# Hybrid mLSTM and sparse-attention decoder layer: gates and convolutions moved under the first projection, page numbers read ahead, the last norm on VectorE alone

## The chip, the core and the metric

One core of a Trainium2 chip runs the whole layer as one program. Its engines each have a queue of their own and meet by semaphores: TensorE (PE in rows; PEld is its weight load), VectorE (DVE), ScalarE (ACT), GpSimd (POOL) and SyncE (SP), which here only issues DMAs. ScalarE and GpSimd issue DMAs too. The metric is the device time of one execution in microseconds (us), lower is better.

## The reference

One inference step of a decoder layer for two groups of tokens with the same weights: a prompt of 1024 tokens, and 8 sampled sequences of 4 new tokens each with 4096 tokens of paged cache. 1056 tokens in all go through every projection.

```
h = rmsnorm(x, nrm[0])
xm, v, ig, fg, og, qn, kvc, kvs, kvw, gn, ga, gb = split_in(h @ p['w_in'])
hm, C, n, m, mconv_new = mlstm_mixer(xm, v, ig, fg, og, mconv, C0, n0, m0, p)
on, new_rows, new_win = nsa_mixer(...)        # compressed, selected, sliding window
merged = sigmoid(ga) * (hm @ p['w_up_m']) + sigmoid(gb) * (on @ p['w_up_n'])
x = x + rmsnorm(merged @ p['w_out'], nrm[1])
...                                            # cross-attention into 256 memory tokens
x = x + rmsnorm((gelu(u) * (h @ p['f_wg'])) @ p['f_wd'], nrm[5])

def mlstm_mixer(xm, v, ig, fg, og, conv_buf, C0, n0, m0, p):
    xc, conv_new = causal_dwconv(xm, conv_buf, p['m_conv_w'], p['m_conv_b'])   # width 4
    xc = silu(xc)
    q, k = xc @ p['m_wq'], xc @ p['m_wk'] * M_HD ** -0.5                       # per head
    i_pre, log_f = ig + b[0], log_sigmoid(fg + b[1])
    ...                                        # chunkwise recurrence, output gate
```

The compressed branch of the sparse attention puts every 32 cached keys and values of each sequence through a two-layer network, which reads the key and value halves of all 32 pages of each of the 8 sequences. Everything is in fp32.

## The kernel before

The layer is a row of stages, each a block of programs for the five engines. A stage ends when all its engines and DMAs are through, and the next begins with none of its own DMAs issued. Inside a stage the order on each engine is written out by hand, and semaphores (`S["..."]`) order the engines.

**front.** The first norm and the input projection. Large products are made exact enough by splitting both operands in a high and a low half and taking three products (`split_product`). The token-major part of the projection comes first. Then 12 chunks of 128 feature rows: for chunk `j`, SP loads the weights into half `j % 2` of `ring`, ScalarE makes the high half (`chunk_high`), VectorE the low half (`chunk_low`), TensorE multiplies, and VectorE drains the product (`drain_chunk`) into `zm` for chunks 0 to 3, the convolution's input, or into `zn`. The halves of chunk 0 lie in `zhalf`, those of the others in two places in `wlow`, which is the same memory as `hm`.

**mlstm.** SP loads gate bias, convolution taps, saved states, the query and key weights of the 4 heads (`wqk`) and the norm's gains. VectorE adds the gate bias and makes the log of the forget gate in four steps, with ScalarE's exponential and logarithm between. It convolves feature tile after feature tile (`convolve(c)`, prompt and sample tokens), with ScalarE's Silu behind each. TensorE projects a head (`project_head`) when its Silu is done, ScalarE copies queries and keys, TensorE turns the keys (`turn_keys`) and ScalarE copies them (`turned_keys`). In between VectorE makes the running maxima, then the carry from tile to tile. ScalarE makes the output gates' sigmoids and then the weights (`weights_ready`). With the weights the scan begins: 8 tiles, in which TensorE, ScalarE, VectorE and GpSimd take turns.

**states and blocks** (`sab_` in names). The mLSTM of the samples, the bias vector of the attention in four parts (`bias_part`, from a one-hot table in `ring`), and the compressed blocks: the prompt's own (`own_first`, which reads pairs that VectorE and ScalarE turn), and those of the 8 sequences, each a first layer for keys and one for values (`first(n, kv)`). Sequence `n` uses buffer `n % 2` of 32 pages. SP, ScalarE and GpSimd load 12, 9 and 11 of them (`load`); for a page an engine first reads its number from `pages` into a register (`value_load`), then issues a DMA of 128 KB. They read four numbers and issue four DMAs in turn, after waiting for the buffer: for sequences 2 and on, the first layers of sequence `n - 2` (`layer1_ready`), for sequence 1 both own first layers (`own1_ready`), since its buffer holds their pairs.

**Sparse attention, merge, output and query, memory, cross-attention** follow and are not touched.

**ff.** The feed-forward, and the last norm on three groups of 352 tokens. For each group TensorE sums squares and spreads the factor row, ScalarE takes the root and copies the row, and the output is scaled by it and added to `x`: VectorE does 6 of the 8 feature tiles (`scale3`, `add3`), GpSimd the other 2 (`finish`). Group 0 is finished while TensorE works on group 2, groups 1 and 2 after the last matmuls.

## Time and profile before

| | us |
|---|---|
| three runs | 2480.99, 2485.36, 2490.33 |
| median | 2485.36 |
| profiled execution | 2488.14 |
| its span in the trace | 2484.9 |

Five stretches of the span, from the trace: busy time of the engines, the clock granted to TensorE as a share of its full 2.4 GHz, and the mean busy share of the 16 DMA engines.

| stretch, us | stage | TensorE | VectorE | ScalarE | GpSimd | clock | DMA |
|---|---|---|---|---|---|---|---|
| 0 to 300 | front | 288.83 | 63.77 | 62.17 | 0.84 | 1.00 | 0.21 |
| 300 to 426 | mlstm | 77.20 | 80.05 | 54.55 | 18.17 | 0.83 | 0.13 |
| 426 to 579 | states and blocks | 119.11 | 33.09 | 18.91 | 47.48 | 0.77 | 0.81 |
| 579 to 2440 | attention to feed-forward | 1781.12 | 885.70 | 549.39 | 351.20 | 0.98 | 0.26 |
| 2440 to 2485 | end of ff | 20.06 | 29.82 | 8.70 | 15.94 | 0.68 | 0.27 |

Over the span TensorE is busy for 2286.3 us (92%), VectorE 1092.4 (44%), ScalarE 693.7 (28%) and GpSimd 433.6 (17%). A row of a timeline gives start and duration, the engine, the line of the program, the operation with what it writes and reads, and in brackets the idle time of the engine before it and what ended it. SPq and ACTq are the queues of an engine that issue DMAs.

### The profile page before, as it was taken

The page shows a single profiled execution, that of the slowest core. Times are in us where ns is not written, and L with a number is a line of the kernel's source. Part 1 is how long each engine was busy: PE and PEld are TensorE (multiplying, and loading weights), DVE is VectorE, ACT ScalarE, POOL GpSimd, SP SyncE. Part 2 cuts the span into 40 slices and gives each one's busy share as a digit, 9 for nine tenths or more (in the row PEclk, how much of TensorE's full clock was granted, in tenths as well). Part 3 has the DMA queues.
Part 4 walks back from the last instruction along what each step waited for, and adds up shares of the span by engine and source line. Part 5 has one row for each costly group of instructions (what it writes and reads, how often), then busy time and mean ns, then how long its engine had stood idle before and what let it go on. Part 6 is the DMA issues. An engine that isn't in the chain of part 4 may idle for free. (4 is left out here: it accounts for less than half of the span.)

```text
span 2484.9 us, 40696 instructions
## 1 busy us (share of the span) xinstructions
PE 2286.3 (92%) x15977; PEld 2076.0 (84%) x15977; DVE 1092.4 (44%) x2456; ACT 693.7 (28%) x1394; POOL 433.6 (17%) x381
## 2 busy tenths in 40 slices
PE   8999875876998998999899999998999999999995
PEld 7799745774555568999899968898999999999995
DVE  2211266134666674132228115457655555552336
ACT  4210153112565563011134003443111111121123
POOL 0000012330322302212011100111221221222223
PEclk9999978788999999999999999998999999999997
DMA  3211111888543523111211055212111111111312
GB/s 141 93 48 51 23 1 43 278 283 317 182 154 103 173 81 108 51 61 47 100 68 35 34 208 227 69 49 73 60 43 52 43 51 43 42 41 45 113 40 77
DMA packets 114298, 233.20 MB, mean 94 GB/s; under 512 B 23394, under 2 KB 76291, under 8 KB 110675
## 3 DMA queue, kind: packets, MB, share of 16 engines
q1 hardware_dynamic: 88250, 183.32, 21.9%
q0 software_dynamic: 10368, 28.33, 3.5%
q10 hardware_dynamic: 15490, 18.97, 2.2%
q8 instruction: 126, 2.06, 0.3%
q14 instruction: 64, 0.52, 0.1%
HBM read 207.28 MB, written 27.47 MB: 94 GB/s over the span
## 5 line engine op out<-in xcount | busy, mean ns | idle before, releaser
L88 PE MATMUL psum<-x_half_high,ff_half 128*128 128x352 f32 x3240 | 790.8, 324 | 10.8 <-POOL ff_half L69 4.9
L88 PEld LDWEIGHTS psum<-x_half_high,ff_half 128*128 128x128 f32 x3240 | 567.0, 189 | 12.8 <-POOL ff_half L69 5.9
L88 PE MATMUL psum<-h_again_low,ff_half 128*128 128x352 f32 x1176 | 378.0, 321 | 0.0
L69 POOL TENSOR_TENSOR ff_half<-ring,ff_half 128x1024 fp32r<-128x1024 f32 (+2 forms) x85 | 177.1, 2083 | 752.5 <-ACT ff_half L3068 752.5
L88 PEld LDWEIGHTS psum<-h_again_low,ff_half 128*128 128x128 f32 x1176 | 222.0, 189 | 0.0
L88 PE MATMUL psum<-merged_high,oq_half 128*128 128x352 f32 x768 | 189.4, 327 | 9.3 <-DVE oq_half L69 7.7
L3068 ACT ACTIVATE ff_half<-ring 128x1024 fp32r<-128x1024 f32 (+2 forms) x88 | 78.0, 888 | 428.2 <-PE psum L88 407.2
L88 PE MATMUL psum<-mid_low,ff_half 128*128 128x352 f32 x516 | 167.0, 324 | 0.0
L88 PEld LDWEIGHTS psum<-merged_high,oq_half 128*128 128x128 f32 x768 | 135.8, 191 | 9.9 <-DVE oq_half L69 8.0
L88 PE MATMUL psum<-h_high,in_half 128*128 128x352 f32 x528 | 126.1, 321 | 0.0
L88 PE MATMUL psum<-x_half_high,mg_w_high 128*128 128x352 f32 x384 | 124.0, 323 | 2.1 <-ACT gated L2135 1.2
L88 PE MATMUL psum<-h_again_low,mg_w_high 128*128 128x352 f32 x384 | 123.1, 321 | 0.0
L88 PE MATMUL psum<-x_half_high,mg_w_low 128*128 128x352 f32 x384 | 123.0, 320 | 0.0
L1761 ACT ACTIVATE na_pt<-psum 128x512 f32<-128x512 f32 (+1 forms) x170 | 86.8, 544 | 94.6 <-PE psum L1636 80.7
L1456 POOL DMA_DIRECT2D na_kv<-in_pool x128 | 70.4, 551 | 226.4 <-PE psum L1663 159.4
L1636 PEld LDWEIGHTS psum<-consts,na_p 128*128 128x128 f32 x528 | 57.6, 144 | 58.7 <-DVE na_p L1919 37.6
L88 PE MATMUL psum<-in_half,h_high 128*128 128x512 f32 (+3 forms) x360 | 102.8, 371 | 0.0
L3392 DVE TENSOR_TENSOR h_again<-h_again,psum 128x352 f32<-128x352 f32 x96 | 49.8, 520 | 119.6 <-PE psum L88 119.5
L1741 ACT ACTIVATE na_p<-na_p,na_nm 128x640 f32<-128x640 f32 (+7 forms) x128 | 92.8, 727 | 28.5 <-DVE na_nm L1777 28.1
L88 PEld LDWEIGHTS psum<-mid_low,ff_half 128*128 128x128 f32 x516 | 98.1, 190 | 0.0
L1636 PE MATMUL psum<-consts,na_p 128*128 128x128 f32 x528 | 80.6, 287 | 15.7 <-DVE na_p L1919 13.0
L855 PE MATMUL psum<-sab_kv,sab_w 128*64 128x128 f32 x1024 | 70.7, 305 | 24.8 <-DMA sab_kv<-in_pool 22.4
(559 smaller groups left out, 4215.8 us busy)
## 6 DMA issues: line engine op xcount, KB each, us to landing
na_kv<-in_pool SPq DMA_DIRECT2D x128, 128.0 KB, 3.5
na_kv<-in_pool POOLq DMA_DIRECT2D x128, 128.0 KB, 4.0
sab_kv<-in_pool SPq DMA_DIRECT2D x96, 128.0 KB, 4.4
mg_w<-in_w_merge SPq DMA_DIRECT2D x15, 768.0 KB, 4.4
sab_kv<-in_pool POOLq DMA_DIRECT2D x88, 128.0 KB, 4.5
ring<-in_f_wu SPq DMA_DIRECT2D x22, 512.0 KB, 3.3
ring<-in_f_wg SPq DMA_DIRECT2D x22, 512.0 KB, 3.2
sab_kv<-in_pool ACTq DMA_DIRECT2D x72, 128.0 KB, 4.5
```

Source lines behind the costliest of these rows:

```text
L69: return engine.tensor_tensor(low, x, high.bitcast(F32), ALU.subtract)
L88: ins = nc.tensor.matmul(out, w[a], x[b], start=first and n == 0, stop=last and n == 2)
L855: last = nc.tensor.matmul(psum[g * HD:(g + 1) * HD, bank, 0:width], w1[:, kv, j, :], rows(g, j), start=(j == 0), stop=(j == CB // 2 - 1))
L1456: eng.dma_start(kv[m % 2][:, b, 2 * PAGE * p:2 * PAGE * (p + 1)], A["pool"][ds(g, 1), :, 2 * PAGE:4 * PAGE].rearrange("a p x -> (a p) x")) ...
L1636: last = nc.tensor.transpose(out[:, c:c + P], src, K["ident"][:, :])
L1741: ins = nc.scalar.activation(x, x, ACT.Exp, bias=nm[:, b, g, i:i + 1], scale=-1.0, accum_out=sums[:, b, g:g + 1])
L1761: nc.scalar.activation(dst, psum[:, 4 + n % 2, 0:2 * m * P], ACT.Copy).then_inc(S["copied"], 1)
L3068: nc.scalar.activation(half(u)[:, 0, 0:n], ring[:, u % 2, 0:n], ACT.Copy).then_inc(S["w_high"], 1)
L3392: ins = nc.vector.tensor_tensor(z[:, f, col(g)], z[:, f, col(g)], bank(v), ALU.add)
```

## The change

**In front.** Gate bias and taps are loaded at the start. The halves of even chunks lie in `zhalf`, those of odd ones in `extra`, so that `hm` is free. VectorE does the gates under chunks 1, 3 and 6, and the convolution of prompt tokens of tile `c` under chunk `4 + c`; ScalarE does the exponential behind the high half of chunk 4, the logarithm behind that of chunk 6 and the four Silus behind those of chunks 7 to 10. At the end SP loads the head weights into the free half of `ring`, where states and blocks finds them too. The small gate tensors and the taps get an earlier place in memory. **In mlstm** the waits for all this go. The sample tokens are convolved all at once (`convolve_sample`) behind the running maxima, and their Silu stands behind the output gates. **In states and blocks** the load of the head weights goes, the one-hot table is loaded after the pages of sequence 0 and the samples' projections, and `bias_part(0)` moves behind `last_entries`. `load` reads three numbers at a time for sequence 0, and for the others all its numbers before it waits for the buffer. **In ff** GpSimd's `finish` goes, and VectorE scales in two halves of 4 tiles and adds all four pairs.

```diff
     def chunk_half(j):
-        if j == 0:
+        if j % 2 == 0:
             return zhalf[:, KD - 2, 0:KD * P], zhalf[:, KD - 1, 0:KD * P]
-        s = 2 * ((j - 1) % 2)
-        return tuple(wlow[:, s + i].rearrange("p n w -> p (n w)") for i in range(2))
+        return tuple(extra[:, i].rearrange("p n w -> p (n w)") for i in range(2))
...
+            sp.wait_ge(S["chunk_low"], nchunk - 1)
+            sp.dma_start(heads_weights(ring), A["m_wqk"]).then_inc(S["wqk_loaded"], 16)
...
             for j in range(2, nchunk):
                 chunk_high(j)
+                if j == 4:
+                    act.wait_ge(S["gate_steps"], 2)
+                    nc.scalar.activation(tmp[:, :, :], tmp[:, :, :], ACT.Exp).then_inc(S["gate_exp"], 1)
+                if j == 6:
+                    act.wait_ge(S["gate_steps"], 3)
+                    nc.scalar.activation(tmp[:, :, :], tmp[:, :, :], ACT.Ln).then_inc(S["gate_ln"], 1)
+                if 7 <= j < 7 + MH:
+                    act.wait_ge(S["conv_ready"], j - 6)
+                    nc.scalar.activation(hm[:, j - 7, 0:TP], hm[:, j - 7, 0:TP], ACT.Silu).then_inc(S["silu_done"], 1)
...
-            for j in range(3):
+            for j in range(2):
                 chunk_low(j)
...
+            under = {1: gate_inputs, 3: one_more, 6: log_forget}
             for j in range(nchunk):
                 drain_chunk(j)
-                if 1 <= j < nchunk - 2:
+                if j < nchunk - 2:
                     chunk_low(j + 2)
+                if j in under:
+                    under[j]()
+                if 4 <= j < 4 + MH:
+                    convolve(j - 4)
...
             def project_head(h):
-                pe.wait_ge(S["silu_done"], h + 1)
...
-            pe.wait_ge(S["steps"], 4)
             nc.tensor.matmul(psum[:, GATE, 0:R], K["tri"][:, :], lf[:, 0:NTILE, :].rearrange("p t h -> p (t h)"),
...
-            pe.wait_ge(S["loaded"], 80)
             project_head(0)
...
+            act.wait_ge(S["conv_ready"], 1)
+            nc.scalar.activation(hm[:, :, TP:T], hm[:, :, TP:T], ACT.Silu).then_inc(S["silu_done"], 1)
             turned_keys(3)
...
         def load(eng, n, first, count, done):
-            if n == 1:
-                eng.wait_ge(S["own1_ready"], 2)
-            if n >= 2:
-                eng.wait_ge(S["layer1_ready"], 2 * (n - 1))
-            for at in range(first, first + count, 4):
-                some = range(at, min(at + 4, first + count))
+            step = count if n else 3
+            for at in range(first, first + count, step):
+                some = range(at, min(at + step, first + count))
                 page = [eng.value_load(pages[0:1, n * NPAGE + e:n * NPAGE + e + 1], min_val=0, max_val=N["n_pool"] - 1) for e in some]
+                if n == 1:
+                    eng.wait_ge(S["own1_ready"], 2)
+                if n >= 2:
+                    eng.wait_ge(S["layer1_ready"], 2 * (n - 1))
...
-            sp.dma_start(wqk[:, :, :, :], A["m_wqk"]).then_inc(S["wqk_loaded"], 16)
...
+            load(sp, 0, 0, SP_N, loaded)
+            sp.wait_ge(S["qk_ready"], 1)
             sp.dma_start(onehot, A["onehot"]).then_inc(S["vec_loaded"], 16)
-            load(sp, 0, 0, SP_N, loaded)
...
             spread_row(a, "diag_a_ready", "arow_ready")
-            bias_part(0)
             own_first(0)
             scores()
             spread_row(M, "diag_m_ready", "mrow_ready")
             last_entries()
+            bias_part(0)
             bias_part(1)
...
+            halves3 = (slice(4, 8), slice(0, 4))
...
-                    scale3(0)
-                    add3(0, pairs[0:3])
+                    scale3(0, halves3)
+                    add3(0, pairs)
             add_square3(7, 2)
-            scale3(1)
+            scale3(1, halves3[0:1])
             mean3(2)
-            add3(1, pairs[0:1])
+            scale3(1, halves3[1:2])
             factor3(2)
-            add3(1, pairs[1:3])
-            scale3(2)
-            add3(2, pairs[0:3])
+            add3(1, pairs)
+            scale3(2, halves3)
+            add3(2, pairs)
```

Order on VectorE. Before, the convolution of tile 0 in mlstm (`low` is the memory of `zm` and `hm`, `xs` and `ys` hold the sample tokens):

```order
L719 TENSOR_SCALAR low<-low,cw 128x1024
L720 TENSOR_SCALAR ys<-xs,cw 128x32
L723 SCALAR_TENSOR_TENSOR low<-low,cw 128x1021
L725 SCALAR_TENSOR_TENSOR ys<-xs,cw,ys 128x32
L723 SCALAR_TENSOR_TENSOR low<-low,cw 128x1022
L725 SCALAR_TENSOR_TENSOR ys<-xs,cw,ys 128x32
L723 SCALAR_TENSOR_TENSOR low<-low,cw 128x1023
L725 SCALAR_TENSOR_TENSOR ys<-xs,cw,ys 128x32
L727 COPY low<-ys 128x32
```

Now, in front under chunks 4 and 5 (L427 drains a chunk, L69 makes a low half):

```order
L427 SCALAR_TENSOR_TENSOR zn<-psum,fr_row 128x1056
L69 TENSOR_TENSOR zn_half<-ring,zn_half 128x1024
L475 TENSOR_SCALAR low<-low,cw 128x1024
L478 SCALAR_TENSOR_TENSOR low<-low,cw 128x1021
L478 SCALAR_TENSOR_TENSOR low<-low,cw 128x1022
L478 SCALAR_TENSOR_TENSOR low<-low,cw 128x1023
L427 SCALAR_TENSOR_TENSOR zn<-psum,fr_row 128x1056
L69 TENSOR_TENSOR tok_half<-ring,tok_half 128x1024
```

The prompt's part moved between a low half and the next drain; the sample's part stands alone later.

Order on ScalarE, in mlstm between the turned keys of head 2 and the weights (`ex`). Before:

```order
L693 ACT_TABLE_LOAD
L693 ACTIVATE branch_gates<-tokn 128x216
L696 ACTIVATE tokm<-tokm 128x512 x8
L696 ACTIVATE tokm<-tokm 32x512
L660 ACTIVATE kt<-psum 128x4x128 x2
L700 ACT_TABLE_LOAD
L700 ACTIVATE ex<-ex 128x128
```

Now:

```order
L725 ACT_TABLE_LOAD
L725 ACTIVATE branch_gates<-tokn 128x216
L728 ACTIVATE tokm<-tokm 128x512 x8
L728 ACTIVATE tokm<-tokm 32x512
L731 ACT_TABLE_LOAD
L731 ACTIVATE low<-low 128x4x32
L700 ACTIVATE kt<-psum 128x4x128 x2
L734 ACT_TABLE_LOAD
L734 ACTIVATE ex<-ex 128x128
```

A table load and the Silu of the sample columns came in ahead of the last turned keys.

Order on TensorE, at the head of states and blocks, from the first row spread to the first page layer (`sab_pairs` are the prompt's pairs, `sab_rel` is the bias table's factor, `sab_kv` a sequence's pages). Before:

```order
L990 MATMUL psum<-sab_tmp,consts 32x128
L998 MATMUL psum<-ring,sab_rel 8x512
L855 MATMUL psum<-sab_pairs,sab_w_3196 64x33 x32
L1041 MATMUL psum<-sab_qT,sab_kT 32x32 x4
L990 MATMUL psum<-sab_tmp,consts 32x128
L1045 MATMUL psum<-sab_Mb,consts 32x8
L998 MATMUL psum<-ring,sab_rel 8x512
L855 MATMUL psum<-sab_pairs,sab_w_3196 64x33 x32
L998 MATMUL psum<-ring,sab_rel 8x512 x2
L855 MATMUL psum<-sab_kv,sab_w_3196 64x128 x32
```

Now:

```order
L1014 MATMUL psum<-sab_tmp,consts 32x128
L879 MATMUL psum<-sab_pairs,sab_w_3197 64x33 x32
L1065 MATMUL psum<-sab_qT,sab_kT 32x32 x4
L1014 MATMUL psum<-sab_tmp,consts 32x128
L1069 MATMUL psum<-sab_Mb,consts 32x8
L1022 MATMUL psum<-ring,sab_rel 8x512 x2
L879 MATMUL psum<-sab_pairs,sab_w_3197 64x33 x32
L1022 MATMUL psum<-ring,sab_rel 8x512 x2
L879 MATMUL psum<-sab_kv,sab_w_3197 64x128 x32
```

The first bias part moved from ahead of the first own-key layer to behind the last entries.

## Rows read from the trace of the kernel before

**Rows 1.** Timeline, VectorE at the mLSTM's start (start us, us, engine, line, op).

```profile
308.08 0.23 DVE L765 TENSOR_TENSOR tokn<-tokn,gb 128x72 f32<-128x72 f32 x1 [7.33 <-DMA mnorm<-in_m_norm]
...
309.37 0.81 DVE L719 TENSOR_SCALAR low<-low,cw 128x1024 f32<-128x1024 f32 x1
...
310.43 1.28 DVE L723 SCALAR_TENSOR_TENSOR low<-low,cw 128x1021 f32<-128x1021 f32 x1
```

**Rows 2.** Timeline, ScalarE before the mLSTM's scan.

```profile
344.96 1.08 ACT L660 ACTIVATE kt<-psum 128x512 f32<-128x512 f32 x2
346.06 1.28 ACT L693 ACT_TABLE_LOAD   x1
347.36 0.38 ACT L693 ACTIVATE branch_gates<-tokn 128x216 f32<-128x216 f32 x1
...
354.68 0.31 ACT L700 ACTIVATE ex<-ex 128x128 f32<-128x128 f32 x1
```

**Rows 3.** Timeline, TensorE, first layers of the pages.

```profile
482.53 5.38 PE L855 MATMUL psum<-sab_kv,sab_w 128*64 128x128 f32 x64
...
506.94 5.42 PE L855 MATMUL psum<-sab_kv,sab_w 128*64 128x128 f32 x64 [6.48 <-DMA sab_kv<-in_pool]
...
519.41 3.71 PE L855 MATMUL psum<-sab_kv,sab_w 128*64 128x128 f32 x64 [0.60 <-DMA sab_kv<-in_pool]
...
524.78 3.71 PE L855 MATMUL psum<-sab_kv,sab_w 128*64 128x128 f32 x64
...
566.07 6.54 PE L855 MATMUL psum<-sab_kv,sab_w 128*64 128x128 f32 x64 [6.89 <-DMA sab_kv<-in_pool]
```

**Rows 4.** Windows of 5 us in states and blocks (busy by engine, PEclk, DMA share, GB/s).

```profile
530.00:535.00 5.00, 0.00 (x0) 0.00 (x0) 1.45 (x3) 0.00 (x0) 2.35 (x5) 0.59 1.04 345
545.00:550.00 5.00, 5.00 (x82) 4.71 (x80) 1.82 (x4) 0.37 (x1) 0.00 (x0) 1.00 0.36 117
```

**Rows 5.** Timeline, the last norm, on TensorE, VectorE and GpSimd.

```profile
2454.58 1.33 PE L2990 MATMUL psum<-consts,ff_acc 128*88 128x1 f32 x8 [3.93 <-DVE ff_acc L3400]
...
2463.52 3.90 DVE L3413 TENSOR_TENSOR h_again<-h_again,ff_row 128x704 f32<-128x704 f32 x2 [0.30 <-ACT ff_row L3130]
...
2467.45 2.24 DVE L3421 TENSOR_TENSOR low<-low,h_again 128x704 f32<-128x704 f32 x1
...
2469.70 1.65 DVE L3421 TENSOR_TENSOR low<-low,h_again 128x704 f32<-128x704 f32 x2
...
2476.30 3.84 DVE L3421 TENSOR_TENSOR low<-low,h_again 128x704 f32<-128x704 f32 x3
...
2466.02 2.93 POOL L3250 TENSOR_TENSOR low<-low,h_again 128x704 f32<-128x704 f32 x1
```

**Rows 6.** Timeline, VectorE's drains under the first projection's chunks.

```profile
195.39 1.26 DVE L411 SCALAR_TENSOR_TENSOR low<-psum,fr_row 128x1056 f32<-128x1056 f32 x1 [9.06 <-PE psum L88]
...
206.83 1.26 DVE L411 SCALAR_TENSOR_TENSOR low<-psum,fr_row 128x1056 f32<-128x1056 f32 x1 [9.06 <-PE psum L88]
```

**Rows 7.** Timeline, TensorE, heads of the mLSTM projected and turned.

```profile
323.04 3.67 PE L539 MATMUL psum<-low,wqk 128*128 128x512 f32 x8 [1.44 <-ACT qT L652]
326.55 1.04 PE L549 MATMUL psum<-consts,kT 128*128 128x128 f32 x8
...
337.50 6.50 PE L539 MATMUL psum<-low,wqk 128*128 128x512 f32 x8 [3.63 <-ACT qT L652]
```

**Rows 8.** Timeline, TensorE at the head of states and blocks.

```profile
431.10 0.64 PE L982 MATMUL psum<-low,sab_wqk 128*128 128x32 f32 x2 [8.13 <-DMA sab_wqk<-in_m_wqk]
...
443.45 3.63 PE L855 MATMUL psum<-sab_pairs,sab_w 128*64 128x33 f32 x64 [1.97 <-ACT sab_pairs L943]
...
456.11 1.87 PE L998 MATMUL psum<-ring,sab_rel 33*8 33x512 f32 x2 [0.68 <-ACT ring L1135]
```

**Rows 9.** Timeline, the DMA issues of pages on SP's and ScalarE's queue.

```profile
473.75 11.44 SPq L937 DMA_DIRECT2D sab_kv<-in_pool  x12
...
530.82 7.35 ACTq L937 DMA_DIRECT2D sab_kv<-in_pool  x9
```

146 lines of the change are left out of this document (65 added, 81 removed).

## Prediction

> **What bounds the kernel now.** I read the shares of the page first: TensorE is busy for 92% of the span, so there is a gain only where it waits. The table of the five stretches shows where: the two in the middle and the last. Then the timeline of each engine there, asking at each gap what ended it.
>
> Between the first projection and the scan of the mLSTM (300 to 359 us) VectorE first waits 7.33 us for a DMA issued at the stage's start, then works off the gates and four convolutions in series [rows 1], and TensorE can project a head only when its convolution is through. What ends this part is ScalarE: behind the turned keys of head 2 it loads a table, takes the gates' sigmoids, turns the last keys, loads the exponential's table and makes the weights [rows 2], for which the scan waits.
>
> In states and blocks (426 to 579) TensorE has 119 us of work in 153 and the DMA engines are 0.81 busy, so neither is full. Each sequence's 4.19 MB of pages come into one of two buffers, and its matmuls start when they are in: at 506.94 and, four sequences on, at 566.07, so 14.8 us each [rows 3]. The DMA rate swings between 345 and 117 GB/s [rows 4]: after a buffer comes free, each queue first reads page numbers.
>
> At the end VectorE's last two groups are one chain, started by the last projection tiles, and these tiles had waited 3.93 us for VectorE's work on the first group [rows 5].
>
> **Gates and convolutions under the chunks.** A chunk takes TensorE 11.44 us: so far apart lie VectorE's drains, and VectorE waits for 9.06 of it [rows 6]. To the drain of 1.26 and a low half of about as much comes at most one convolution, 0.81 + 3 x 1.28 = 4.65 us [rows 1], and items of 0.2: 7.2 in all. The low half stands ahead of the convolution, so the next chunk doesn't wait for it. Free, with 4 us to spare; without that cover it would be 19 us. ScalarE now waits for VectorE before the exponential, the logarithm and each Silu, with the next chunk's high half queued behind; each of these inputs is made at least one chunk before, so these waits and the three table loads lie in its idle time. The loads that moved into SP's queue (gate bias, taps, head weights) have nothing urgent behind them, and the head weights' half of the ring is free from chunk 10's low half on, 30 us before they are read.
>
> The new head: TensorE starts at 300.0 with the two cumulative products (about 1.1), then per head 3.67 us of projection and 1.04 of turns [rows 7]. ScalarE needs 3.1 per head (two copies of 1.0 and 1.08), so TensorE sets the pace: 300.0 + 1.1 + 4 x 3.67 + 3 x 1.04 + 0.6 of small turns = 319.5, and ScalarE ends the keys of head 2 at 320.6. Before, it ended them at 346.04 and the weights at 354.99 [rows 2], 8.95 later. Into that chain comes a Silu of the sample's columns with its table load, 1.28 + 0.28. Weights at 320.6 + 8.95 + 1.56 = 331.1: **23.9 us earlier**. VectorE isn't late: the running maxima are done by 308, the sample's convolution (some 21 small instructions) by 312, and its carry chain ends at about 324. The scan is untouched.
>
> Bounds: 26 if the small turns hide; below, TensorE at half clock throughout: a head then takes 6.50 [rows 7] and its turns double, 3.8 us more a head, 15 in all, which leaves 9.
>
> The Trainium skill, "ScalarE: Activation LUTs", section "What ACT_TABLE_LOAD costs", adds a drain of some 1.38 us to each load, 2.66 in all. The trace disagrees: behind the load at 346.06 the next activation starts at 347.36, 1.30 later [rows 2]. By the page the term would be 22.5.
>
> **States and blocks, its head.** TensorE no longer waits for the head weights, 426.4 instead of 431.10. But the first own-key layer waits for ScalarE's turned pairs until 443.45 [rows 8], and those stand behind 5 DMA issues and 9 pages on ScalarE's queue, as before: the 4.7 us go into a longer wait. Bias part 0, which filled that wait, now stands behind the last entries, on the path, and part 1 waits for its copy: 1.87 less 0.07 of overlap, and a wait of 0.68 like the one now ahead of part 3 [rows 8]. So the **first page layer is 2.5 us later**. SP's new wait, for the projections, has the one-hot table, the states and sequence 1's pages behind it; SP comes to it at about 443, and the projections are done at 435: nothing. The table then has 5 us to land.
>
> **Its pages.** SP's 12 pages took 11.44 us; ScalarE's 9 began 2.3 us after the buffer was free (528.49, then 530.82) and took 7.35 [rows 3, 9]. These 2.3 are four page numbers, 0.57 each. SP and GpSimd now read theirs ahead of the release: their first issue comes at once, and SP's 12 take (11.44 - 8 x 0.57) = 7 us. ScalarE comes to its reads only with the release, since the layer's activation stands ahead of them: its first page is later (9 x 0.57 = 5.1), its last at the same 10 us.
>
> The queues then issue faster than the engines move, and the rate is what the trace shows at its fullest, 345 to 348 GB/s, of which 345 has its row [rows 4]: 12.1 us for 4.19 MB. From release to start I take 0.5 + 12.1 + 2 to land = 14.6 (ScalarE's last page gives 10 + 4.5). Before, it was 19.0, from 482.53 + 5.38 to 506.94 [rows 3]. A warm sequence computes from 519.41 to 528.49, 9.1 [rows 3]. A pair needs the larger of 9.1 + 14.6 = 23.7 and 2 x 12.1 = 24.2, against 29.6. So sequence 3 starts at 487.9 + 14.6 = 502.5, 4.4 earlier, and sequence 7 four steps of 12.1 on, at 550.9, 15.2 earlier. Its first layer took 6.54 at half clock after a wait of 6.89 [rows 3]; after 2 us of waiting I take the 3.71 of a warm one, 2.8 less. 15.2 + 2.8 - 2.5 = **15.5 us**.
>
> Bounds: below, sequences stay 14.8 apart and only the bias counts: -2.5. Above, the 23.7 of the cycle and a hidden bias: 19.
>
> **The last norm.** Beside GpSimd's add, one of VectorE's pairs takes 2.24; alone, two take 1.65, so 0.83 each [rows 5]. Alone, a group is two scales of 1408 columns (1.55 each) and four adds: 6.4 us, where three quarters took 3.90 + 3.84 = 7.7. Group 0 ends 1.3 earlier, and TensorE's last tiles with it. Groups 1 and 2 took 2463.52 to 2480.14, 16.6; now 2 x 6.5 = 13.0, the factor row of group 2 (2.0 on TensorE, 0.5 on ScalarE) hidden behind the adds of group 1, which it wasn't. 1.3 + 3.6 less 0.3, as four stores now come faster than they drain: **4.6**. Bounds: 2.5 (only the contention goes) and 6.5 (TensorE's last 24 matmuls at full clock).
>
> Sum: 23.9 + 15.5 + 4.6 = 44.0. The profiled execution took 2488.14 us, 2484.9 of it span, and would take 2444.1. It lay 2.8 above the median of the runs, 2485.36; for the median I forecast 2441.
>
> **Rivals.** (a) The page reads were no cost: the pages come as fast as the engines move them. The Trainium skill, "DMA: Bandwidth & Descriptors", section "Issuing engines are not separate DMA queues", calls the sequencer's time to initiate usually small beside the DMA. In rows: sequences stay 14.8 apart, the term is -2.5, 2485.4 - 23.9 + 2.5 - 4.6 = 2459. Against it stand the 117 GB/s between loads [rows 4]. (b) TensorE stays at half clock in the new head of the mLSTM: 15 lost, 2456. Against it: it leaves the chunks at full clock and rests 1.6 us. (c) More: sequences 11.8 apart, the bias hidden, the last tiles warm, 50: 2435. (d) Slower: VectorE's convolution makes the next chunks' halves late. It decides from 11.44 us of VectorE work in a chunk on; each of four chunks then stalls TensorE by the excess. Slower than before needs 11 us of excess, a convolution of 15 for 4.65; with one of 19, 15 in excess, it is 2441 + 60 = 2501. Two inputs in SBUF beside a busy GpSimd more than doubled an add [rows 5], but GpSimd is idle under the chunks. (e) It doesn't do what it says: the stage's start waits for another load and the pages stay late, with the norm alone gaining: 2481.
>
> **How the numbers follow.** Forecast 0.58, (a) 0.10, (b) 0.10, (c) 0.15, (d) 0.03, (e) 0.04. The range takes in (c) and (b) with the 5 us by which runs scatter: 2431 to 2457. A measurement here tells 0.5%, 12.4 us, from no change. Faster is all but (d) and (e): 0.93; same 0.04; slower 0.03.
>
> **What would show it.** Right: drains still 11.44 apart with convolutions between; TensorE's first matmul of the mLSTM at 300, a head in 3.67; weights near 331; 19.4 us from the first own-key layer to the first page layer (it was 16.9); sequences 12 apart at 345 GB/s, no pause in SP's 12 issues; last adds of 0.83. Wrong: chunks that stretch, sequences 14 apart, the first page layer no later, or a new wait in the sparse attention behind.

## The result, and the profile after

Four executions of the changed kernel took 2451.59, 2456.33, 2457.59 and 2457.59 us, median 2456.96; four of the kernel before, median 2486.44 (2480.99 to 2490.33). The ratio is 0.9872, with a 95% interval from 0.9858 to 0.9887: 28 to 35 us faster. The forecast of 2441 was 16 us too low, and the time lies at the very end of the range. The change works, at two thirds of the gain that was forecast.

The profiled execution is the fastest of the four (span 2449.9 us), so the ledger below, trace against trace, closes at 35.0 us and not at the 29.5 of the medians. Each line is the time between two landmarks, after minus before.

| part | predicted, us | traces, us |
|---|---|---|
| the front ends (last drain 298.40, now 299.43) | 0 | +1.0 |
| weights of the mLSTM (354.99, now 331.98), all up to there | -23.9 | -23.0 |
| first own-key layer (443.45, now 420.76), all up to there | -23.9 | -22.7 |
| from it to the first page layer (16.90, now 20.98) | +2.5 | +4.1 |
| from there to the end of the stage's last matmul (117.7, now 110.5) | -18.0 | -7.2 |
| from there to group 0's factor in the last norm: no change made | 0 | -3.3 |
| from the factor to the end (41.0, now 35.2) | -4.6 | -5.8 |
| sum | -44.0 | -35.0 |

The -3.3 us in untouched stages are scatter: in the profiled executions of all 14 kernels that stretch takes 1860.8 to 1865.8 us, with no clear order in it. One line of the ledger is far off, the pages: 10.8 us short, where the whole ledger is 9.0 short (the scatter and the norm give some back) and the medians are 14.5 short of 44.0.

**Front and mLSTM.** The timeline of VectorE under chunks 5 and 6 (start us, us, engine, line, operation) answers to [rows 6] and [rows 1]: drain, low half, convolution, and the next drain 11.49 us later. VectorE still waits 4.42 of them.

```profile
230.59 1.26 DVE L427 SCALAR_TENSOR_TENSOR zn<-psum,fr_row 128x1056 f32<-128x1056 f32 x1 [4.30 <-PE psum L88]
231.76 1.22 DVE L69 TENSOR_TENSOR tok_half<-ring,tok_half 128x1024 fp32r<-128x1024 f32 x1
232.90 0.81 DVE L475 TENSOR_SCALAR low<-low,cw 128x1024 f32<-128x1024 f32 x1
233.74 3.93 DVE L478 SCALAR_TENSOR_TENSOR low<-low,cw 128x1021 f32<-128x1021 f32 x3
242.08 1.26 DVE L427 SCALAR_TENSOR_TENSOR zn<-psum,fr_row 128x1056 f32<-128x1056 f32 x1 [4.42 <-PE psum L88]
```

The timeline of ScalarE ahead of the scan, against [rows 2]: the new table load and Silu take 1.51 from the end of the sigmoids, as reckoned, and the load's next activation again starts 1.3 later.

```profile
321.41 1.28 ACT L725 ACT_TABLE_LOAD   x1
322.71 0.38 ACT L725 ACTIVATE branch_gates<-tokn 128x216 f32<-128x216 f32 x1
323.00 4.77 ACT L728 ACTIVATE tokm<-tokm 128x512 f32<-128x512 f32 x9
327.78 1.28 ACT L731 ACT_TABLE_LOAD   x1
329.07 0.31 ACT L731 ACTIVATE low<-low 128x128 f32<-128x128 f32 x1
329.29 1.06 ACT L700 ACTIVATE kt<-psum 128x512 f32<-128x512 f32 x2
330.37 1.28 ACT L734 ACT_TABLE_LOAD   x1
331.67 0.31 ACT L734 ACTIVATE ex<-ex 128x128 f32<-128x128 f32 x1
```

On TensorE the first two heads read as follows, against [rows 7]:

```profile
301.45 5.38 PE L585 MATMUL psum<-low,ring 128*128 128x512 f32 x8
...
306.77 3.60 PE L585 MATMUL psum<-low,ring 128*128 128x512 f32 x8
```

The first head runs mostly at half clock (5.38) behind a rest of 1.62 us, those after it take 3.60, so rival (b) is out but for 1.7 us. Even that is not constant: of the eleven profiled kernels with this front, all with the same rest of 1.62, the first head takes 5.4 us in seven and 3.68 in four (e2, e4, e10, e12 below). And the stage began late. The difference is there from the program's start, in SP's queue and on TensorE; first of the kernel before, where the load of the first weights begins at 1.35, and then of the changed one:

```profile
1.35 2.13 SPq L209 DMA_DIRECT2D ring<-in_w_tok  x4
...
9.54 4.01 PE L241 MATMUL psum<-fr_unit,tokm 128*128 128x9 f32 x18 [9.54 <-DMA consts<-in_consts]
```

```profile
1.35 0.42 SPq L214 DMA_DIRECT2D gb<-in_gate_b  x1
1.81 0.43 SPq L215 DMA_DIRECT2D cw<-in_m_conv  x1
2.29 2.57 SPq L211 DMA_DIRECT2D ring<-in_w_tok  x4
...
10.60 4.01 PE L248 MATMUL psum<-fr_unit,tokm 128*128 128x9 f32 x18 [10.60 <-DMA consts<-in_consts]
```

The gate bias and the taps went ahead of the first weights on SP, 0.94 us of issue, and the first matmul, which waits for `consts` from ScalarE's queue, comes 1.06 later. The prediction said that these loads "have nothing urgent behind them". In the profiles of the experiments it starts at 9.30 and 9.40 in the two kernels with the old front, and at 10.2 to 10.6 in the ten with the new one. That these two loads are the cause was not tried by itself.

**States and blocks.** TensorE, against [rows 8] and [rows 3]: the first own-key layer, bias part 0, the first page layer, then the layers of sequences 3, 5 and 7.

```profile
420.76 3.63 PE L879 MATMUL psum<-sab_pairs,sab_w 128*64 128x33 f32 x64 [9.03 <-ACT sab_pairs L968]
...
427.05 1.87 PE L1022 MATMUL psum<-ring,sab_rel 33*8 33x512 f32 x2 [1.46 <-DMA ring<-in_onehot]
...
441.74 5.77 PE L879 MATMUL psum<-sab_kv,sab_w 128*64 128x128 f32 x64 [2.37 <-ACT sab_act_own L1193]
...
485.40 6.12 PE L879 MATMUL psum<-sab_kv,sab_w 128*64 128x128 f32 x64 [4.27 <-DMA sab_kv<-in_pool]
...
514.08 5.45 PE L879 MATMUL psum<-sab_kv,sab_w 128*64 128x128 f32 x64 [5.94 <-DMA sab_kv<-in_pool]
...
541.39 5.38 PE L879 MATMUL psum<-sab_kv,sab_w 128*64 128x128 f32 x64 [1.94 <-DMA sab_kv<-in_pool]
```

Bias part 0 waits 1.46 us for the one-hot table, which was to have "5 us to land": it was issued at 420.25 behind 32 pages and landed 6.8 later. That is most of the 1.6 by which the head is later than reckoned. Sequences 3 to 7 start 14.0 us apart (14.8 before, 12.1 forecast). The 7.2 us of the pages come from three places: 2.9 up to sequence 3, 3.1 in the four steps from there to sequence 7, and 1.2 in the layers of sequence 7.

**The last norm**, on VectorE, against [rows 5]: scales of 1408 columns in 1.6, four adds in 3.30, groups 1 and 2 from 2433.06 to 2446.02. That is 12.96 us, where 13.0 were forecast and 16.6 were taken. Group 0 is finished 1.3 sooner. The remaining 0.8 of this term is behind the last add: the span ends 3.9 after it, 4.7 before.

```profile
2433.06 1.63 DVE L3419 TENSOR_TENSOR h_again<-h_again,ff_row 128x1408 f32<-128x1408 f32 x1 [0.30 <-ACT ff_row L3149]
...
2434.67 1.61 DVE L3419 TENSOR_TENSOR h_again<-h_again,ff_row 128x1408 f32<-128x1408 f32 x1
...
2436.32 3.30 DVE L3429 TENSOR_TENSOR low<-low,h_again 128x704 f32<-128x704 f32 x4
2439.53 3.15 DVE L3419 TENSOR_TENSOR h_again<-h_again,ff_row 128x1408 f32<-128x1408 f32 x2
2442.72 3.30 DVE L3429 TENSOR_TENSOR low<-low,h_again 128x704 f32<-128x704 f32 x4
```

### The profile page after: what moved, and what is told of

Same layout as the page of the kernel before. It is cut to its first block and busy times, and to the rows that moved or that the text cites. A ratio compares the mean times of both kernels' runs of the same rounds, so it can differ in the third digit from the quotient of the medians.

```text
span 2449.9 us, 40689 instructions
## 1 busy us (share of the span) xinstructions
PE 2282.5 (93%) x15977; PEld 2073.6 (85%) x15977; DVE 1087.6 (44%) x2456; ACT 695.6 (28%) x1396; POOL 418.3 (17%) x375
## 5 line engine op out<-in xcount | busy, mean ns | idle before, releaser
L69 POOL TENSOR_TENSOR ff_half<-ring,ff_half 128x1024 fp32r<-128x1024 f32 (+2 forms) x85 | 177.5, 2089 | 749.6 <-ACT ff_half L3087 749.6
L1765 ACT ACTIVATE na_p<-na_p,na_nm 128x640 f32<-128x640 f32 (+7 forms) x128 | 92.8, 727 | 28.0 <-DVE na_nm L1801 27.8
L1660 PE MATMUL psum<-consts,na_p 128*128 128x128 f32 x528 | 79.5, 285 | 15.9 <-DVE na_p L1943 13.1
L3366 DVE TENSOR_TENSOR ff_cv<-ff_cv,ff_row 128x352 f32<-128x352 f32 x66 | 68.8, 1042 | 56.1 <-ACT ff_cv L3133 56.1
L69 POOL TENSOR_TENSOR mg_w_low<-mg_w,mg_w_high 128x1536 fp32r<-128x1536 f32 x15 | 53.8, 3584 | 201.5 <-DVE mg_w_high L65 195.4
```

The lines of the kernel that those rows point to most:

```text
L69: return engine.tensor_tensor(low, x, high.bitcast(F32), ALU.subtract)
L1660: last = nc.tensor.transpose(out[:, c:c + P], src, K["ident"][:, :])
L1765: ins = nc.scalar.activation(x, x, ACT.Exp, bias=nm[:, b, g, i:i + 1], scale=-1.0, accum_out=sums[:, b, g:g + 1])
L3366: nc.vector.tensor_tensor(c, c, row[:, g, :], ALU.mult).then_inc(S["factored"], 1)
```

## The experiments

The first four take the change apart and try the most obvious culprit. "Less than the kernel before" is by the ratio, with its interval in brackets. Stretches and starts are from one profiled execution of each kernel. The release of a buffer is the end of the first layers that read it.

**e1_pages**, before with the read-ahead alone (the diff is the `load` of the change, nothing else).

> The kernel before with one part of the change: the page numbers are read ahead (three at a time for sequence 0, all of an engine's before its wait for the others). The prediction's theory (the reads cost, the engines take 345 GB/s) put this part at 18 us with no bias part moved: sequences 3 and 7 would start 12 us a sequence apart, 2468. In the changed kernel the same part gave little: from the first page layer (441.74) to the stage's last matmul (551.85) are 110.1 us, where it was 117.3 before, so 7.2 us. Theory A (what holds the pages back is elsewhere: ScalarE's nine reads behind the release, the rate of the DMA engines, the cold layer behind each wait) expects that here as well: 7 us less than before, sequences 13.7 apart, about 2479. Rival B (the head of the stage in the changed kernel took the gain away) expects 12 us a sequence here and 2470 or less.

Measured: 2479.03, ratio 0.9984 [0.9973, 0.9995]: 4.0 us less [1.2, 6.7]. From the first page layer to the end of the stage's last matmul 111.3 us for 117.7, sequences 3 to 7 13.8 apart. Theory A holds: the read-ahead gives 6.4 us in that stretch with the old head, 7.2 with the new.

**e2_front**, the changed kernel with `load` and the norm as before.

```diff
-            step = count if n else 3
...
+            for at in range(first, first + count, 4):
...
+            for g in range(NG):
+                finish(g)
```

> The changed kernel with the page reads and the last norm as before: gates and convolutions under the chunks, the head weights in the ring and the bias part moved are left. If the three parts add up as in the two traces (22.7 us up to the first own-key layer, 4.1 lost behind it up to the first page layer, pages as before), this one is 18.6 us faster than the kernel before, 2468. If the first page layer's 4.1 us are hidden again by the pages, which then start their cycle from the same DMA stream, it is 22.7 faster, 2464.

Measured: 2464.42, ratio 0.9926 [0.9908, 0.9944]: 18.4 us less [13.9, 22.9]. Own-key layer to page layer 21.0, page layer to end 118.0 (117.7 before): the head's loss is the new head's own, and nothing hides it. The first of the two expectations (18.6) is met, but the interval does not exclude the second.

**e3_norm**, before with the norm on VectorE alone.

> The kernel before with the last norm on VectorE alone. The prediction: 4.6 us less, groups 1 and 2 in 13.0 us where they took 16.6, group 0 1.3 us earlier: about 2482. The traces of before and after differ by 5.8 us behind group 0's factor (29.2 to 35.0), of which 0.9 lie behind the last add: 2481. If GpSimd's share had been worth its work, no difference, 2486.

Measured: 2479.80, ratio 0.9986 [0.9976, 0.9996]: 3.5 us less [1.0, 6.0]. In its trace groups 1 and 2 take from 2461.27 to 2474.24, 12.97. The term is right. The three parts alone give 4.0 + 18.4 + 3.5 = 25.9 against 31.8 together, a difference of 5.9 that the intervals together allow: no dependence of one part on another is shown, and one of this size is not excluded.

**e4_act_reads**, ScalarE's numbers read between its two activations.

```diff
                 gelu(n, 0)
...
+                if n + 2 < NSEQ:
+                    early = read_pages(act, n + 2, range(SP_N, SP_N + ACT_N))
                 gelu(n, 1)
...
-                    load(act, n + 2, SP_N, ACT_N, loaded)
+                    load(act, n + 2, SP_N, ACT_N, loaded, early)
```

> The changed kernel, and ScalarE reads its nine page numbers for sequence n + 2 between the two activations of sequence n, so that its DMAs can be issued at the release, too. Theory A1 (ScalarE's reads hold the pages back: in the changed kernel its first page of sequence 3 is issued 4.8 us after the release and its last 10.1 after it, and the layer starts 6.7 later): from release to layer 14.5 us instead of 16.8, sequences 12.5 apart instead of 13.7, 6 us less over seven sequences, 2451. Theory A2 (the DMA engines are the limit: they moved 330 to 341 GB/s in most of these windows, and in the pause at a release they still have the other buffer's pages): the layers start when they did, 2457. Theory A3 (the cold first layer of 5.4 to 6.1 us behind a wait, for 3.7, and the buffer's turn): a shorter wait gives back as much, 2455.

Measured: 2453.31, ratio 0.9883 [0.9865, 0.9900], not told apart from the changed kernel's 0.9872. ScalarE issues at once now (its nine of sequence 3 from 468.82 to 475.12, where it was 473.57 to 478.66), and the layer starts no earlier: 17.5, 16.4 us after the release for sequences 3 and 7, sequences 14.1 apart. A1, as the one cause, falls. ScalarE's pages had been the last to land in the changed kernel; now SP's are, at the time when ScalarE's were (table below).

The next four: fewer bytes, a warm TensorE, an earlier head, a finer release.

**e5_half**, of sequences 2 to 7 only the keys' half of each page is loaded.

```diff
-                    eng.dma_start(kv_in[n % 2][:, e, :], A["pool"][ds(g, 1), :, 0:2 * PAGE]
+                    eng.dma_start(kv_in[n % 2][:, e, 0:(1 if n >= 2 else 2) * PAGE], A["pool"][ds(g, 1), :, 0:(1 if n >= 2 else 2) * PAGE]
```

> The changed kernel, but of the pages of sequences 2 to 7 only the keys' half is fetched (64 KB for 128 KB in each DMA, as many DMAs and page numbers; the first layers for values read what the buffer held). Theory A2 (the pages' time is the rate of the DMA engines, shared by the two buffers in flight): from release to layer falls from 16.3 to 20.6 us to about 10, the first layers no longer wait except after a cold start, and the stage's part from the first page layer to the end falls from 110.5 to about 85 us, where TensorE's own work sets it. Theory A4 (what costs is the issue of the DMAs or a fixed latency of each, not their bytes): it stays above 105.

Measured: one run, 2443.93. Page layer to end 99.7 us, neither 85 nor 105: with half the bytes sequences 3 to 7 are still 12.8 apart. So bytes cost something, and something else sets a floor just below. One candidate is in GpSimd's timeline:

```profile
484.28 6.37 POOL L962 DMA_DIRECT2D sab_kv<-in_pool  x11 [6.37 <-issue]
496.71 6.37 POOL L962 DMA_DIRECT2D sab_kv<-in_pool  x11 [6.06 <-issue]
509.43 6.37 POOL L962 DMA_DIRECT2D sab_kv<-in_pool  x11 [6.35 <-issue]
```

Its eleven DMAs of a sequence take 6.37 us and the eleven numbers of the next another 6.1 to 6.4, back to back: 12.4 to 12.7 a sequence. "issue" says that it waited for no release, only for itself. SP is the other candidate, and the later of the two: from its first DMA of sequence 3 to its last of sequence 7 it waits for no release at all, and of sequences 4 to 7 its last page lands 0.2 to 2.4 us after GpSimd's. In the changed kernel at full size GpSimd still waits for a release in every second sequence, for 9 us:

```profile
481.97 6.38 POOL L962 DMA_DIRECT2D sab_kv<-in_pool  x11 [6.35 <-issue]
497.55 6.56 POOL L962 DMA_DIRECT2D sab_kv<-in_pool  x11 [9.20 <-PE psum L879]
510.28 6.38 POOL L962 DMA_DIRECT2D sab_kv<-in_pool  x11 [6.17 <-issue]
```

**e6_warm**, unread matmuls ahead of the page layers of sequences 3, 5, 6 and 7.

```diff
             for n in range(3, NSEQ):
+                if n != 4:
+                    pe.wait_ge(S["copied"], n)
+                for _ in range({3: 9, 5: 13, 6: 3, 7: 4}.get(n, 0)):
+                    nc.tensor.matmul(psum[:, 2, 2 * P:4 * P], K["ident"][:, :], w1[:, 0, 0:4, :].rearrange("p j d -> p (j d)"), start=True, stop=True)
                 first(n, 0)
```

> The changed kernel with 9, 13, 3 and 4 small matmuls that nobody reads (128 x 256, some 0.44 us each at full clock) ahead of the page layers of sequences 3, 5, 6 and 7, so that TensorE doesn't rest before them. If the granted clock falls because TensorE waits, these first layers take 3.7 us instead of 5.4 to 6.1, the next buffer is free 1.7 to 2.4 us earlier in each pair, and the stage ends 4 to 6 us earlier: 2452. If the clock falls for another reason, or the DMA engines set the pace anyway, nothing: 2457. If the small matmuls run past the landing of the pages, up to 3 us slower.

Measured: 2454.97, ratio 0.9889 [0.9861, 0.9917]: no gain. Behind the small matmuls the layers of sequences 3, 5 and 6 take 3.71 us, for 6.12, 5.45 and 5.38; behind the four ahead of sequence 7 and a wait of 2.17 the layer still takes 5.38. Sequences are 14.1 apart. The run is not a clean test of the warm layers, since the small matmuls ran past the pages: those of sequence 5 had landed at 514.0 and those of sequence 6 at 527.7, and the layers came 3.7 and 1.8 later.

```profile
511.90 5.88 PE L1147 MATMUL psum<-sab_w,consts 128*128 128x256 f32 x26
517.71 3.71 PE L879 MATMUL psum<-sab_kv,sab_w 128*64 128x128 f32 x64
```

**e7_head**, another order at the head of the stage.

```diff
-            load(act, 0, SP_N, ACT_N, loaded)
             turn_pairs(nc.scalar.copy, 1)
...
             nc.scalar.activation(kw[:, :, :], heads(psum[0:NS, 4, :]), ACT.Copy, scale=k).then_inc(S["qk_copied"], 1)
+            load(act, 0, SP_N, ACT_N, loaded)
...
-            load(sp, 0, 0, SP_N, loaded)
+            load(sp, 0, 0, 3, loaded)
             sp.wait_ge(S["qk_ready"], 1)
             sp.dma_start(onehot, A["onehot"]).then_inc(S["vec_loaded"], 16)
+            load(sp, 0, 3, SP_N - 3, loaded)
```

> The changed kernel with another order at the head of states and blocks: ScalarE turns its pairs and copies the sample's queries and keys before it issues its nine pages of sequence 0, and SP loads the one-hot table behind its first three pages instead of behind all twelve. In the changed kernel TensorE waits 9.03 us for ScalarE's turned pairs behind those pages, then 1.46 for the one-hot table. Theory B (this head sets when the first page layer starts, and what the read-ahead saves behind it doesn't depend on it): the first own-key layer starts near 412 instead of 420.8, then ScalarE's bias copies behind its pages (till about 422) hold the second: first page layer at 434 to 436 instead of 441.7, 6 to 7 us less in all, 2450. Rival (sequence 0's pages land late instead, since ScalarE issues its share 4 us later): 3 us or less.

Measured: 2449.29, ratio 0.9855 [0.9834, 0.9876], beside the changed kernel's 0.9872 [0.9858, 0.9887]: the median gains 7.7 us, the ratio 4, and the intervals of the two overlap. In the trace the stage begins at 406.10 (ScalarE's first DMA; 403.15 in the changed kernel), and counted from there the first page layer is 7.7 us earlier and the last matmul 4.0. So the order is worth some 4 to 8 us, by these figures; behind it the pages take part of it back, 114.3 from page layer to end for 110.5.

**e8_split**, each page in two DMAs, so that the keys' half of a buffer is free one layer earlier.

```diff
+                for kv in parts:
...
+                    if n >= 2:
+                        eng.wait_ge(S["layer1_ready"], 2 * (n - 2) + kv + 1)
+                    c = slice(kv * PAGE, (kv + 1) * PAGE)
...
+                        eng.dma_start(kv_in[n % 2][:, e, c], A["pool"][ds(g, 1), :, c].rearrange("a p x -> (a p) x")
+                                      ).then_inc(done[n % 2][kv], 16)
```

> The changed kernel with each page in two DMAs of 64 KB, keys and values: the keys' half of a buffer is released after the first layer for keys and not only after that for values, 3.7 to 5.4 us earlier, ScalarE issues the keys' part between its two activations with the numbers kept for the values'. If the buffer's release bounds the cycle (from release to layer 17 and two layers of 11 in a pair of 28, while 8.4 MB need 24 at 345 GB/s), a pair falls to 24 or 25 us: 9 us less, 2448. If DMAs with rows of 512 bytes move less than those of 1 KB, or twice as many issues (12 + 12 on SP, 6 us each) are too many, a pair takes more than 28 us and the kernel is slower than 2457.

Measured: 2480.32, ratio 0.9979 [0.9969, 0.9989]: 23 us slower than the changed kernel by the medians, 133 us from page layer to end. The windows of the DMA engines at their fullest (columns as in [rows 4]):

```profile
510.00:515.00 5.00, 2.24 (x26) 2.24 (x28) 1.76 (x3) 0.00 (x0) 0.82 (x2) 0.83 1.09 281
545.00:550.00 5.00, 0.00 (x0) 0.00 (x0) 0.63 (x2) 0.37 (x1) 4.62 (x9) 0.75 1.10 299
```

They are as busy as in [rows 4] and move 281 and 299 GB/s for 345, with rows of 512 bytes and DMAs of half the size: about a sixth of the rate is gone. But over the stretch of the row below they are busy 0.84 of the time, at 228 GB/s, while SP works without a break:

```profile
480.64 92.28 SPq L964 DMA_DIRECT2D sab_kv<-in_pool  x120
```

SP waits for no release in these 92.28 us, GpSimd only once after sequence 3 has begun (its other pauses are "issue", its own numbers), and the values' layers of sequences 5, 6 and 7 start within 0.1 us of the landing of SP's last page. Here the queues are what sets the pace; the lower rate comes on top.

The last four: the two edits that did nothing alone, together; half the bytes without ScalarE's late reads; one sequence in flight at a time; and all that helped.

**e9_warm_reads**, e4's and e6's edits (9, 10 and 8 small matmuls ahead of sequences 3, 5 and 7).

> The changed kernel with both edits that gave nothing alone: ScalarE reads its page numbers ahead, and small matmuls (9, 10 and 8) keep TensorE busy ahead of the page layers of sequences 3, 5 and 7. With ScalarE's reads ahead the DMA engines moved 340 to 350 GB/s for 20 us on end, then almost nothing for 5 (63 and 91 GB/s at 495 to 500) until TensorE was through sequence 3; so a pair there was TensorE's 11.0 us for a cold sequence, plus 17.5 from its release to the next layer. Theory A2 in this form (a pair is the two in series, and each edit alone moved the limit to the other): a warm sequence takes 9.2, a pair 26.7 and not 28.7, and the stage ends about 5 us earlier than with the reads alone: 2450. Rival: the landing moves on to where it was, whatever TensorE does, as in the two runs alone: 2455.

Measured: 2453.97, ratio 0.9877 [0.9862, 0.9892]: no gain. Page layers of 3, 5 and 7 warm (3.71), sequences 13.7 apart. The rival is right: the landing moves to where it was. The buffers of sequences 5 and 7 come free at 496.3 and 525.1, but SP is still at its numbers and issues their first pages at 500.2 and 529.2; it waits for no release in its 66.1 us. (Ahead of sequence 5 the small matmuls ran past the pages again, by 2.8 us.)

**e11_half_reads**, e5 with ScalarE's reads ahead.

> Half of each page for sequences 2 to 7, as before (keys only, 64 KB in a DMA), now with ScalarE's numbers read ahead. With half the bytes alone sequences stayed 12.9 us apart for 13.65, and ScalarE's last page was issued 9.3 us after the release. If at half the bytes ScalarE's reads are what holds the pages (while at full size the DMA engines hide them), sequences now come 11 us apart, which is TensorE's own work with one or two cold layers: from the first page layer to the end 88 us for 99.7. If it is a cost of each DMA, or of the release, they stay 12.9 apart.

Measured: one run, 2442.17; 98.6 us from page layer to end, sequences 12.6 apart. Not ScalarE's reads, then, at half the bytes either. GpSimd's bursts start 12.4 to 12.7 apart as in e5, but SP's, which waits for no release, start 13.1 to 14.0 apart and 4.3 to 7.9 us behind the release, and for sequences 5 to 7 the layer starts less than 0.1 us after SP's last page and 1.5 to 2.7 after GpSimd's.

**e12_hold**, SP and GpSimd wait for the landing of the sequence before.

```diff
+                if n >= 2 and first != SP_N:
+                    eng.wait_ge(loaded[(n - 1) % 2], 16 * ((SP_N + ACT_N) * ((n - 1) // 2 + 1)))
                 for e, g in zip(some, page):
                     eng.dma_start(kv_in
```

> The changed kernel, but SP and GpSimd issue a sequence's pages only when SP's and ScalarE's pages of the sequence before have landed, too. The prediction reckoned a buffer's load at the full 345 GB/s from its release; in the changed kernel two buffers' loads are in flight at once from 480 on. Theory A2 (they share the rate, and the earlier one lands later for it): the odd sequences, whose buffer is released 12 to 17 us after the other, start 14.5 to 15.5 us after their release instead of 16.3 to 17.2, the even ones later; the DMA engines pause for some 2 us a sequence, and in all 0 to 6 us slower. Rival (a DMA's time from issue to landing doesn't depend on what else is under way): the odd ones start as late as before, 16.8 after the release.

Measured: 2463.52, ratio 0.9913 [0.9898, 0.9929], some 6.5 us slower than the changed kernel by the medians, 10 by the ratios. The odd sequences start 19.0 to 20.7 us after their release, not 14.5 to 15.5. From GpSimd's first issue to the layer it is 13.5 to 16.8 for sequences 3 to 7, mean 15.2, so a load alone takes about what the prediction gave it, and in this run waiting for a turn costs more than the company of a second load. As a test of the shared rate it is inconclusive, since ScalarE's share was not held.

**e10_all**, e4, e6 and e7 together (matmuls as in e9), and the Silu of the sample columns as a sigmoid with the gates and a product on VectorE:

```diff
-            nc.scalar.activation(hm[:, :, TP:T], hm[:, :, TP:T], ACT.Silu).then_inc(S["silu_done"], 1)
...
+            nc.scalar.activation(ys[:, :, :, :].rearrange("p c b t -> p c (b t)"), hm[:, :, TP:T], ACT.Sigmoid).then_inc(S["silu_done"], 1)
...
+            nc.vector.tensor_tensor(hm[:, :, TP:T], hm[:, :, TP:T], ys[:, :, :, :].rearrange("p c b t -> p c (b t)"), ALU.mult)
```

> The edits of the run before this one, the new order at the head of states and blocks (which gave 7.7 us up to the first page layer and 4.0 at the stage's end), and the sample columns' Silu made as a sigmoid on ScalarE, in the table that is loaded for the gates, and a product on VectorE, so that one of the three table loads ahead of the mLSTM's weights goes. In the prediction the Silu and its table load were 1.56 us on the chain to the weights. If that holds, the weights are ready 1.3 us earlier than the changed kernel's 331.98, and in all 2457 - 1.3 - 4 to 7 - 3 = 2446. If the DMA engines take back what the head gives, 2450.

Measured: 2446.98, ratio 0.9841 [0.9827, 0.9854], about 8 us faster than the changed kernel by the ratios, whose intervals do not overlap, and the fastest kernel here with right results. ScalarE ahead of the scan:

```profile
321.98 4.77 ACT L730 ACTIVATE tokm<-tokm 128x512 f32<-128x512 f32 x9
326.65 1.04 ACT L700 ACTIVATE kt<-psum 128x512 f32<-128x512 f32 x2
327.71 1.28 ACT L734 ACT_TABLE_LOAD   x1
329.01 0.31 ACT L734 ACTIVATE ex<-ex 128x128 f32<-128x128 f32 x1
```

From the last of the sigmoids' group to the exponential there is one table load for two. Counted from TensorE's first matmul of the stage (301.49, 301.01 in the changed kernel), the weights are ready 3.1 us earlier: 1.3 of it the table load, and the rest the first head, which ran at full clock here, as in e2, e4 and e12, and so not by this edit.

## What held the pages: two loops of one length

This is SP's work for sequences 3 to 7, 60 page numbers and 60 DMAs, and what SP waited inside this row (waits: total us, times, longest us), in the kernel before:

```profile
490.30 71.56 SPq L937 DMA_DIRECT2D sab_kv<-in_pool  x60
...
SPq L935 <- PE psum L855: 5.2, 2, 2.6
```

and in the changed kernel:

```profile
468.77 63.81 SPq L962 DMA_DIRECT2D sab_kv<-in_pool  x60
...
SPq L962 <- PE psum L879: 1.0, 2, 0.8
```

In 63.8 us SP waits 1.0. The other 62.8 are its own work: 48 numbers (those of sequence 3 were read ahead of the row) at 0.57 are 27.4, which leaves 0.59 for each of 60 DMAs, so 13.9 for the numbers and DMAs of one sequence. After its last DMA of sequence 3 (issued at 475.0) the first of sequence 4 comes at 482.5, 2.7 after the release of its buffer; that of sequence 6 comes at 511.1, with the buffer free since 507.05. Reading ahead hides numbers only in time that the queue would have waited. Counted with the wait just ahead of the row, that was 7.5 us in these five sequences and is 4.4 now: 3.1 less, and sequence 7 comes 3.1 us sooner after sequence 3. **The first loop is SP's queue: 2 x 13.9 = 27.8 us for a pair of sequences**, against the 24.2 that the prediction let the DMA engines set.

The second loop goes through the buffer. SP is late for the even sequences only; for 3, 5 and 7 its first DMA comes 0.2 us after the release, and still the layer starts 16.8, 17.2 and 16.3 after it. Their last pages to land are ScalarE's, which reads its nine numbers behind the release. The ends of the last packets of each queue, by the trace of the DMA engines:

| sequence | changed: layer | SP's last | ScalarE's last | e4: layer | SP's last | ScalarE's last |
|---|---|---|---|---|---|---|
| 3 | 485.4 | 481.9 | 484.8 | 486.2 | 485.5 | 483.1 |
| 5 | 514.1 | 511.4 | 513.5 | 515.3 | 514.4 | 511.7 |
| 7 | 541.4 | 537.6 | 540.9 | 542.7 | 541.7 | 541.2 |

From the release to the layer are 16.8 us in the mean, and the sequence's own layers then take 11.0 to 11.5 until the buffer is released again. **Together that is 28.0 from sequence 3 to 5 to 7, within 0.2 us of the first loop.** That fits edits to one of them having given nothing. With ScalarE's reads ahead (e4) SP's pages are the last, and no earlier, since SP's 12 DMAs of sequence 3, now beside ScalarE's, take 8.4 us for 6.9. With a warm TensorE as well (e9) SP comes 3.9 and 4.1 us late to sequences 5 and 7. In the changed kernel an earlier release can win little more than the 1.0 us that SP still waits. With SP's part made longer (e8), the pace follows it.

The rate of the DMA engines has a share in both loops: from SP's last issue of a sequence to the end of its last packet are 6.4 to 8.9 us, and 1.5 to 3.0 with half the bytes (e11), where sequences come 12.6 apart. In the changed kernel the engines are busy 0.93 of the time from sequence 3 to sequence 7 and move 291 GB/s. What fewer pages on SP would give, with ScalarE's reads ahead, was not run, so how the time divides between issue and rate stays open.

## Why the prediction was right, and where it was wrong

- **Gates and convolutions: right.** Drains stay 11.4 to 11.6 apart, the weights are 23.0 earlier for 23.9. TensorE starts at 301.0 for 300.0. The loads put first in SP's queue, to which the prediction gave no cost ("nothing urgent behind them"), fit this, though they were not tried alone. From that start to the keys of head 2 it takes 20.4 us for the 20.6 reckoned, with 1.7 of half clock in it: the sum was that much too long where it ran warm (the two cumulative products take 0.4 for 1.1), and the two errors nearly cancel.
- **Silu and table load, 1.56: right** (1.51; without one of the loads, 1.3 less).
- **First page layer +2.5: right in kind, 4.1 in size.** The term that was mis-sized is the one-hot table's. The wait for the one-hot table was left out: it was given 5 us to land and took 6.8, behind the 32 pages.
- **Pages, -18.0: wrong, -7.2.** The step that failed is "A pair needs the larger of 9.1 + 14.6 = 23.7 and 2 x 12.1 = 24.2". A third term is missing from it, the queue's own round. "SP's 12 take (11.44 - 8 x 0.57) = 7 us" is right (6.7 to 7.3), but the reads had only moved, behind the DMAs of the sequence before, and a pair of rounds is 27.8. The rows for it were there: 11.44 for 12 DMAs and 8 numbers [rows 9], and 4 more numbers, 13.7, for 13.9 measured. The first term was too small as well. For 14.6 from release to layer it is 16.3 to 17.2 in sequences 3, 5 and 7: ScalarE's last page takes 5.9 to 7.0 from issue to landing, for 4.5. And for the 9.1 of a warm sequence it is 11.0 to 11.5 in 3 and 5, since their first layers run partly at half clock. Last, "after 2 us of waiting I take the 3.71 of a warm one": sequence 7 waited 1.94 and its first layer took 5.38, so 1.2 of that 2.8 came. The prediction had named "sequences 14 apart" as a sign of being wrong, and it is what came. That the total still fell inside the range, by 0.04 us, is luck.
- **Rival (a), 2459, had almost the right time for another reason.** Its rule, the Trainium skill's "DMA: Bandwidth & Descriptors", section "Issuing engines are not separate DMA queues", calls the time to initiate usually small beside the DMA. For one DMA the trace agrees: 0.59 us of issue beside 4.8 from issue to landing (median on SP). The conclusion that the rival drew from it does not hold here, since the issues and numbers of a round add up: SP's queue worked for 62.8 of 63.8 us. Sequences did not stay 14.8 apart either.
- **The last norm, -4.6: right** (-5.8). The 1.3 and 3.6 came as reckoned (1.3 and 3.7); the 0.3 that it took off for the stores has the wrong sign: the span ends 0.8 sooner behind the last add. Alone, four adds take 3.30, 0.83 each, as [rows 5] had it. In [rows 5] GpSimd's add runs from 2466.02 to 2468.95 and VectorE's, begun at 2467.45, ends 0.74 after it, as if it had waited for the whole of it. The Trainium skill's "SBUF — State Buffer", section "🔬 SBUF: two separate sides", calls the port pair that the two share an exclusive lock held for a whole instruction; the trace agrees.
- **Rival (b)** cost 1.7 us in one head of this execution and nothing in others, (d) nothing, as the 4.4 us of rest under each convolution show.

## What to carry to other kernels

Work that is moved ahead of a wait is free only as far as its queue would have waited: add up all that the queue does in one round, reads and issues, and compare that with the round's length first. When several edits to different engines each give nothing, look for the engine that never waits, and measure the length of every loop: two of one length hide each other. And before a small load is put first in a queue, look at what stands behind it there.

## What was not expected of the hardware

- A page number costs its queue about as much as the 128 KB DMA that it addresses: 0.57 us for 0.59 on SP (0.50 in sequence 2, 0.70 in sequence 3 of e4, where ScalarE issues from the same moment), and on GpSimd eleven of each take 6.1 to 6.4 and 6.4.
- Page DMAs of half the size, with rows of 512 bytes, brought the engines, equally busy, from 345 down to 281 and 299 GB/s (e8).
- Nine small matmuls in a wait, and the page layer behind them ran at a granted clock of 2.4 GHz and took 3.71 us even with 2.43 us of waiting left (e6, sequence 3). Behind bare waits of 1.4 to 5.9 us the layers of sequences 3, 5, 6 and 7 took 5.4 to 6.1 in the changed kernel, partly at 1.2 GHz; behind four small matmuls and 2.17 us of waiting one took 5.38 (e6, sequence 7). It gained nothing here.
- The same rest of 1.62 us ahead of the mLSTM's first head was followed by 5.4 us, mostly at 1.2 GHz, in seven profiled executions and by 3.68 us in four.
